# S5 table steps: both sums behind the four products, kernel products ahead of the transposes, forget-gate maps and value copies on ACT

## Chip, cores and metric

One core of one Trainium2 chip. The metric is the device time of one execution in microseconds; the number compared is the median of several runs. Engines: PE is TensorE (matmuls and transposes), ACT is ScalarE, DVE is VectorE, POOL is GpSimd, SP is the engine that only issues transfers here.

## What is computed

A trunk of two residual layers over 512 tokens of width 1024, all in float32. Layer 0 projects the normalised input once (`proj = hn @ w_in`) and feeds an HGRN2 mixer (a gated linear recurrence) and a Mamba-2 mixer; layer 1 has an S5 mixer (a complex diagonal state-space model) and a top-2-of-8 expert SwiGLU. What the change touches is the forget gate of HGRN2 and the preparation of S5:

```python
def hgrn2_mixer(q_pre, ff_pre, fb_pre, i_pre, g_pre, lb, norm_w):
    q = silu(q_pre); v = i_pre
    log_lb, log_1m_lb = log(maximum(lb, LB_FLOOR)), log1p(-lb)
    def forget(f_pre):
        logf = logaddexp(log_lb, log_1m_lb + log_sigmoid(f_pre))
        return logf, -expm1(logf)          # logarithm of the forget gate, and the key
    ...
def _s5_one_direction(ug, a_re, a_im, log_step, b_re, b_im, c_re, c_im):
    # lam = exp(a * delta), one complex number for each of 64 groups x 64 states
    # states by an associative scan over time, outputs from them by c
    ...
```

With s the sigmoid of the pre-activation, the forget gate is `lb + (1 - lb) * s` and the key is `(1 - lb) * (1 - s)`: an affine map each, with a scale and an offset for every channel. The logarithm of the gate is taken after it.

The S5 layer is computed in chunks of 8 time steps. For that the kernel needs, for each of the 64 groups, tables of powers of lam times b (input maps, called BP), powers of lam times c (output maps, CP), and their products (the 15 kernel taps inside a chunk). All depend on parameters alone.

## The kernel before

The order of work is written out by hand; each engine has one in-order program, and they meet on semaphores (`wait_ge`, `then_inc`).

**Blocks and steps.** The first five groups of the projection (ff, fb, q, v, g: forget gates forward and backward, query, value, output gate) are cut into 20 blocks, numbered by `slot`, of 8 block products each (a 128 x 128 weight against 512 columns). The trace shows a block product as two matmul records at L1318. From product 52 (in block 6) to product 160 the table steps of the S5 layer, k = 0 to 31, are threaded between the block products: step k comes ahead of product 52 + floor(k x 108 / 32), thus every 3 or 4 products. A step handles two of the 64 groups.

**A step on DVE** (`powers(k)`): L2837 and L2841 are the two products of BP (512 columns), L2846 adds them; L2850 and L2855 are the two products of CP (576 columns), L2861 adds them. BP and CP have two buffers each, used in turn. BP(k) waits for PE to have transposed and multiplied step k - 2. CP(k) waits for the stores of CP(k - 2) to have landed (`s_cst`). The products are followed by a wait for themselves (`chain.settle()`) ahead of each sum. Behind steps 2 to 5 and 11 to 14 stand four more operations (`logs_in`: the key's map L2816, the gate's map L2818, and the two halves of a split for the logarithm, L2823 and L2825), behind steps 10 and 19 a sum of 2048 columns (`logs_out`, L2829), and behind four later steps the copy of one value block from PSUM (`v_copy`, L2870).

**A step on PE** (`s5_step`): in every fourth step four transposes of a block of C (`c_block`, L1353); then `b_step(k)`, four transposes of BP (L1364); then `kernel_step(k - 1)`, eight small products of BP and CP (L1375).

**A step on ACT**: in every fourth step copies of the C block (`c_copies`, L2153); then two stores of CP(k - 1) (`c_store`, L2182), the copy of the transposed BP (`b_copy`, L2161), its store (L2165), two copies of the kernel taps (`kernel_copy`, L2173) and their store (L2188). At steps 8 and 17 the two logarithms stand behind (`logs`, L2129 and L2130). When the steps of a block are through, `dense_drain(slot)` takes the block's result out of PSUM: two sigmoids for a forget gate (L2120, L2121), Silu for the query (L2123), sigmoid for the output gate (L2125), nothing for the value, which DVE copies. Behind the drain of block 4 ACT copies the first decay tables (L2140), and behind that of block 5 the last ones (L2142, L2143); PE's first C transposes wait for these, and block 6 is behind them in PE's order.

**What follows.** When block 19 is drained, the decay scans of the HGRN2 mixer begin, on ACT (L2262), POOL (L1109, L1112), DVE (L3028) and PE.

**Transfers.** SP loads the weights of the projection in tiles of 1 MB into a ring of six; two tiles are released at about every fourth block's end. The stores of the steps go over ACT's queue.

Of the kernel before, what the change touches and what calls it, by code (L numbers as in the profile page):

```python
# [10 lines left out]
ALU = mybir.AluOpType  # L11
# [42 lines left out]
def build_program(nc, I, out):  # L54
# [27 lines left out]
    with ctx:  # L82
# [68 lines left out]
        add_group("v", w_in, c_v, 512, "tok", "D")  # L151
# [70 lines left out]
        s_k = sem("key_ready")  # L222
# [805 lines left out]
        def _(pool):  # L1028
# [119 lines left out]
            pool.wait_ge(s_lb, HEADS + 1)  # L1148
# [97 lines left out]
        def _(pe):  # L1246
# [76 lines left out]
            def s5_step(k):  # L1323
# [5 lines left out]
                b_step(k)  # L1329
                if k:  # L1330
                    kernel_step(k - 1)

# [125 lines left out]
            def hg_spread(hd):  # L1458
                pe.wait_ge(s_lb, hd + 2)
# [601 lines left out]
        def _(act):  # L2061
# [49 lines left out]
            def dense_drain(slot):  # L2111
# [79 lines left out]
            for slot in range(SLOTS):  # L2191
                for k in steps_of[slot]:
                    if k % 4 == 1 and k < NSTEP - 4:
                        c_copies(k // 4 + 1)
                    if k:
                        c_store(k - 1)
                    b_copy(k)
                    if k:
                        b_store(k - 1)
                        kernel_copy(k - 1)  # L2200
# [15 lines left out]
                elif slot == 5:  # L2216
# [4 lines left out]
                    c_copies(0)  # L2221

# [423 lines left out]
        def _(dve):  # L2646
# [69 lines left out]
            chain.link(dve.tensor_tensor(hgc[:, 7, :], hgc[:, 4, :], hgc[:, 5, :], ALU.subtract))  # L2716
            chain.settle()
# [95 lines left out]
            def logs_in(d, b):  # L2813

                dve.wait_ge(s_drA, cumA[gidx[("ff", "fb")[d]]])
                dve.tensor_scalar(kT[d][:, b, :], kT[d][:, b, :], hgc[:, 6, b:b + 1], hgc[:, 7, b:b + 1],  # L2816
                                  ALU.mult, ALU.add).then_inc(s_k, 1)
                chain.link(dve.tensor_scalar(lf[d][:, b, :], lf[d][:, b, :], hgc[:, 6, b:b + 1], hgc[:, 5, b:b + 1],  # L2818
                                             ALU.mult, ALU.add))
                chain.settle()  # L2820
                if d:
                    dve.wait_ge(s_lf, 1)
                chain.link(dve.tensor_scalar(lnb4[:, b, :], lf[d][:, b, :], 1.0 / LN_SPLIT, 1.0, ALU.mult, ALU.min))  # L2823
                chain.settle()
                dve.tensor_scalar(lf[d][:, b, :], lf[d][:, b, :], LN_SPLIT, None, ALU.max).then_inc(s_lnin, 1)  # L2825
# [5 lines left out]
            def powers(k):  # L2831
# [829 lines left out]
```

## Time and profile before

| | |
|---|---|
| median of 3 runs | 2614.95 us (2611.85 to 2617.03) |
| the profiled execution | 2610.64 us, span 2608.8 us |
| busy share of the span | PE 94%, DVE 65%, ACT 49%, POOL 9% |
| mean granted clock of TensorE | 0.975 of full speed |
| first step's product on DVE (L2837) | 66.69 us |
| last table operation on DVE (L2861) | 229.36 us |
| span of the stretch in question | some 169 us of 2608.8 |

How to read it: the profile is one execution, its times in us from the start of the span. A row of the timeline is one instruction or several merged ones (x2, x8) in order of time. Behind it stands in brackets how long the engine was idle before it and what it waited for. A wait is put down to the event that came last.

### The profile page before, as it was taken

The numbers are of one execution on the slowest core, as the hardware profiler recorded it, in microseconds if no ns is written. First come the engines' busy times: TensorE is split into PE (matmuls) and PEld (weight loads), VectorE is DVE, ScalarE is ACT, GpSimd is POOL, SyncE is SP. The second block draws the span as 40 slices with busy tenths as digits, with TensorE's granted clock in tenths as the row PEclk, the third lists the DMA queues.
The fourth block names the chain that finished last, engine by engine and source line by source line (L and its number), as shares of the span: only waits on it lengthen the run. The fifth ranks groups of instructions, "written<-read, shape, count | busy, mean of one in ns | idle before, by whom it ended". The sixth has DMA issues, their size and how long they took to land.

```text
span 2608.8 us, 31697 instructions
## 1 busy us (share of the span) xinstructions
PE 2458.2 (94%) x12566; PEld 1978.6 (76%) x12566; DVE 1684.6 (65%) x2051; ACT 1281.0 (49%) x1489; POOL 222.5 (9%) x236
## 2 busy tenths in 40 slices
PE   7889998999999999679799999999999999999987
PEld 4445545488888887678599888998899988998866
DVE  6897687322223344693566788668876688667865
ACT  3434434122222223652356676666765577656753
POOL 4114725000000000000100000000000000000010
PEclk9999998999999999789799999999999999999998
DMA  6556411343322223433387799778997799777961
GB/s 169 174 166 203 118 65 41 103 150 96 98 97 98 97 98 113 163 146 106 108 289 242 262 369 354 253 249 296 369 314 249 248 347 369 263 249 263 375 247 50
DMA packets 316386, 526.14 MB, mean 202 GB/s; under 512 B 19286, under 2 KB 175546, under 8 KB 313578
## 3 DMA queue, kind: packets, MB, share of 16 engines
q1 hardware_dynamic: 287162, 479.73, 53.2%
q0 software_dynamic: 5888, 25.78, 3.2%
q10 hardware_dynamic: 23184, 18.55, 2.2%
q8 instruction: 102, 1.67, 0.3%
q14 instruction: 50, 0.41, 0.0%
HBM read 494.46 MB, written 45.81 MB: 207 GB/s over the span
## 4 chain that ended last, share of the span: by engine, by line
PE 81%; DVE 10%; ACT 2%; DMA 2%; issue 2%; POOL 2%; ACTq 0%; POOLq 0%; DVEq 0%
PE psum L1891 28%; PE psum L1405 17%; PE psum L1951 12%; PE psum L1716 5%; PE psum L1953 5%; PE psum L1318 3%; PE psum L1293 2%; PE psum L2051 2%; PE psum L1489 1%; DVE stages L859 1%; DMA s_output_maps_by_state<-stages 1%; DVE stages L869 1%; DVE stages L864 1%; DVE stages L860 1%; POOL stages L1109 1%
## 5 line engine op out<-in xcount | busy, mean ns | idle before, releaser
L3500 DVE TENSOR_TENSOR stages_r<-kept,stages_r 128x2048 fp32r<-128x2048 f32 x336 | 769.3, 2291 | 239.7 <-ACT stages_r L2499 238.5
L2499 ACT ACTIVATE stages_r<-kept 128x2048 fp32r<-128x2048 f32 x336 | 637.6, 1912 | 218.6 <-PE psum L1891 104.1
L1891 PE MATMUL psum<-stages_r 128*128 128x512 f32 x3136 | 738.8, 393 | 3.2 <-issue 3.2
L1891 PEld LDWEIGHTS psum<-stages_r 128*128 128x128 f32 x3136 | 583.7, 188 | 127.0 <-issue 4.8
L1951 PE MATMUL psum<-stages_r 128*128 128x320 f32 x1792 | 465.9, 346 | 4.1 <-DVE stages L3533 3.1
L1405 PE MATMUL psum<-stages_r 128*128 128x512 f32 x1920 | 437.5, 390 | 3.2 <-ACT stages_r L2078 2.7
L1953 PE MATMUL psum<-stages_r 128*128 128x160 f32 x1792 | 423.6, 236 | 0.0
L1405 PEld LDWEIGHTS psum<-stages_r 128*128 128x128 f32 x1920 | 359.9, 188 | 79.5 <-ACT stages_r L2078 3.1
L1953 PEld LDWEIGHTS psum<-stages_r 128*128 128x128 f32 x1792 | 343.5, 192 | 2.0
L1951 PEld LDWEIGHTS psum<-stages_r 128*128 128x128 f32 x1792 | 337.7, 188 | 6.8 <-DVE stages_r L3500 3.8
L3152 DVE TENSOR_TENSOR stages_r<-kept,stages_r 128x2048 fp32r<-128x2048 f32 x54 | 123.8, 2292 | 338.6 <-ACT stages_r L2357 338.6
L2357 ACT ACTIVATE stages_r<-kept 128x2048 fp32r<-128x2048 f32 x54 | 103.5, 1917 | 325.8 <-PE psum L1405 219.1
L1716 PE MATMUL psum<-stages_r,stages_front_r 128*128 128x512 f32 x672 | 152.6, 389 | 0.8 <-issue 0.8
L1716 PEld LDWEIGHTS psum<-stages_r,stages_front_r 128*128 128x128 f32 x672 | 126.1, 188 | 27.3 <-issue 1.2
L1318 PE MATMUL psum<-stages,kept 128*128 128x512 f32 x256 | 118.8, 609 | 0.0
L2537 ACT ACTIVATE stages<-stages 128x160 f32<-128x160 f32 x112 | 37.8, 338 | 159.5 <-DVE stages L3533 159.5
L1318 PEld LDWEIGHTS psum<-stages,kept 128*128 128x128 f32 x256 | 46.9, 192 | 53.8 <-issue 53.8
L1196 POOL DMA_INDIRECT stages<-moe_rows_by_token,stages x8 | 12.3, 1539 | 868.4 <-PE psum L1899 520.4
L3536 DVE TENSOR_TENSOR kept<-stages 128x160 f32<-128x160 f32 x112 | 36.6, 327 | 45.2 <-ACT stages L2537 45.2
L2064 ACT ACTIVATE stages<-kept 128x1024 f32<-128x1024 f32 x24 | 25.3, 1055 | 77.5 <-DVE kept L3146 49.9
L1489 PE MATMUL psum<-stages,kept 128*128 128x512 f32 x128 | 59.4, 594 | 0.0
L1293 PE MATMUL psum<-kept,stages 128*128 128x512 f32 x128 | 57.7, 613 | 0.8 <-DVE stages L3139 0.8
(439 smaller groups left out, 2470.0 us busy)
## 6 DMA issues: line engine op xcount, KB each, us to landing
kept<-in_moe_w_gu_dram SPq DMA_DIRECT2D x224, 1024.0 KB, 7.1
kept<-in_moe_w_down_dram SPq DMA_DIRECT2D x112, 1024.0 KB, 6.5
kept<-in_ffn_w_gu_dram SPq DMA_DIRECT2D x28, 1024.0 KB, 5.2
kept<-in_ev_w_in_dram SPq DMA_DIRECT2D x16, 1024.0 KB, 7.3
kept<-in_ffn_w_down_dram SPq DMA_DIRECT2D x14, 1024.0 KB, 5.0
s_output_maps_by_state<-stages ACTq DMA_DIRECT2D x64, 128.0 KB, 2.0
s_input_maps<-stages ACTq DMA_DIRECT2D x32, 256.0 KB, 2.5
s_output_maps<-s_output_maps_by_state SPq DMA_DIRECT2D x32, 256.0 KB, 4.9
```

What stands on the lines that cost most here:

```text
L1293: m = pe.matmul(psum[:, b0 + b, 0:width], act[:, 4 * kk + k, b * P:(b + 1) * P], w[:, k, 0:width], **at)
L1318: m = pe.matmul(psum[:, b, :], *pair, start=kk == 0 and k == 0, stop=kk == 1 and k == 3)
L1405: m = pe.matmul(psum[:, 4 * (g % 2) + b, :], *pair, start=kk == 0 and k == 0 and n == 0, stop=kk == 1 and k == 3 and n == 2, skip_group_ch ...
L1489: m = pe.matmul(bank, w[:, k, b * P:(b + 1) * P], hnT[:, n, :], **at)
L1716: m = pe.matmul(psum[:, 2 * c + hf, :], a[:, k, at], w[hf][:, k, :], start=j == 0 and k == 0 and n == 0, stop=j == FJ - 1 and k == 3 and n ...
L1891: m = pe.matmul(out_, a, b, start=start and n == 0, stop=stop and n == len(pairs) - 1, skip_group_check=True)
L1951: pe.matmul(bank[:, 0:2 * CAP], wh[:, k, fs], x_[:, k, :], start=k == 0, stop=False, skip_group_check=True)
L1953: m = pe.matmul(bank[:, 0:CAP], wl[:, k, fs], x_[:, k, 0:CAP], start=False, stop=k == 7, skip_group_check=True)
L2357: act.activation(f_high[t % 2], ring[:, n % RING, :].rearrange("p (k n) -> p k n", k=4), ACT.Copy).then_inc(s_wh, 1)
L2499: act.activation(w_high[n % WSLOTS], unit_tile(n), ACT.Copy).then_inc(s_wh, 1)
L3152: dve.tensor_tensor(f_low[t % 2], ring[:, (SPLIT_RUNS[run][1] + t) % RING, :].rearrange("p (k n) -> p k n", k=4), f_high[t % 2], ALU.subtr ...
L3500: dve.tensor_tensor(w_low[n % WSLOTS], unit_tile(n), w_high[n % WSLOTS], ALU.subtract).then_inc(s_ws, 1)
```

## The change

It moves work and reorders it; nothing is computed that was not before.

- `powers(k)`: all four products come first, then the sum of BP, then the sum of CP. A wait for the finished sum of the step before stands ahead of each second product, since BQ and CQ, the scratch buffers of the second products, are single.
- `logs_in` becomes `logs_of`: its two split operations are put inside the next step's `powers`, one behind the BP products and one behind the CP products (steps 3 to 6 and 12 to 15).
- The two affine maps of `logs_in` go to ACT as `bounded_forget(d, b)`, behind the drains of blocks 4 to 11 (and behind the decay copies in blocks 4 and 5).
- The value copies go to ACT as drains of blocks 12 to 15.
- PE does `kernel_step(k - 1)` ahead of `b_step(k)`, and ACT does `kernel_copy(k - 1)` ahead of `b_copy(k)`.

```diff
-        add_group("v", w_in, c_v, 512, "tok", "D")
+        add_group("v", w_in, c_v, 512, "tok", "A")
...
                     c_block(k // 4 + 1)
-                b_step(k)
                 if k:
                     kernel_step(k - 1)
+                b_step(k)
...
                 name, bank = groups[g][0], psum[:, b, :]
-                if name == "v":
-                    return
                 act.wait_ge(s_grp, 4 * g + b + 1)
...
+                elif name == "v":
+                    act.wait_ge(s_lam, 16)
+                    act.activation(vtok[:, b, :], bank, ACT.Copy).then_inc(s_drA, 1)
...
+            def bounded_forget(d, b):
+
+                act.wait_ge(s_lb, 2)
+                act.wait_ge(s_drA, cumA[gidx[("ff", "fb")[d]]] - 3 + b)
+                act.activation(lf[d][:, b, :], lf[d][:, b, :], ACT.Identity, scale=hgc[:, 6, b:b + 1], bias=hgc[:, 5, b:b + 1])
+                act.activation(kT[d][:, b, :], kT[d][:, b, :], ACT.Identity, scale=hgc[:, 6, b:b + 1], bias=hgc[:, 7, b:b + 1]).then_inc(s_k, 1)
...
                     if k:
                         c_store(k - 1)
+                    if k:
+                        kernel_copy(k - 1)
                     b_copy(k)
                     if k:
                         b_store(k - 1)
-                        kernel_copy(k - 1)
...
                     c_copies(0)
+                if 4 <= slot < 12:
+                    bounded_forget(slot // 4 - 1, slot % 4)
...
-            def logs_in(d, b):
...
+            def logs_of(d, b):
+
+                split_done = []
+
+                def logs_split():
+                    dve.wait_ge(s_k, 4 * d + b + 1)
+                    if d:
+                        dve.wait_ge(s_lf, 1)
+                    chain.link(dve.tensor_scalar(lnb4[:, b, :], lf[d][:, b, :], 1.0 / LN_SPLIT, 1.0, ALU.mult, ALU.min))
+                    split_done.append(chain.n)
+
+                def logs_floor():
+                    dve.wait_ge(chain.sem, split_done[0])
+                    dve.tensor_scalar(lf[d][:, b, :], lf[d][:, b, :], LN_SPLIT, None, ALU.max).then_inc(s_lnin, 1)
+
+                return logs_split, logs_floor
...
-            def powers(k):
+            def powers(k, behind=None):
...
+                if k:
+                    dve.wait_ge(s_bc, 2 * k - 1)
...
-                chain.settle()
-                dve.tensor_tensor(BP[k % 2], BP[k % 2], BQ, ALU.add).then_inc(s_bc, 1)
+                inputs_done = chain.n
+                if behind is not None:
+                    behind[0]()
                 dve.wait_ge(s_cc, k // 4 + 1)
...
+                if k:
+                    dve.wait_ge(s_bc, 2 * k)
...
-                chain.settle()
+                outputs_done = chain.n
+                if behind is not None:
+                    behind[1]()
+                dve.wait_ge(chain.sem, inputs_done)
+                dve.tensor_tensor(BP[k % 2], BP[k % 2], BQ, ALU.add).then_inc(s_bc, 1)
+                dve.wait_ge(chain.sem, outputs_done)
                 dve.tensor_tensor(CP[k % 2], CP[k % 2], CQ, ALU.add).then_inc(s_bc, 1)
...
-                powers(k)
+                powers(k, logs_behind)
+                logs_behind = None
...
-                        logs_in(d, k - LOGS_IN[d])
+                        logs_behind = logs_of(d, k - LOGS_IN[d])
...
-                for b in range(4):
-                    if k == steps_of[4 * gv + b + 1][0]:
-                        v_copy(b)
```

The semaphore `s_lb` gets one more increment, behind the last of the four constants of the maps (`hgc`), and its later waits count one further; one more wait between these constants and the table work goes.

## Rows read from the trace of the kernel before

**Rows 1.** Timeline of DVE, step 3 with logarithms: start, length, engine, line.
```profile
88.46 0.69 DVE L2837 TENSOR_TENSOR stages<-stages,kept 128x512 f32<-128x512 f32 x1
89.06 0.69 DVE L2841 TENSOR_TENSOR stages<-stages 128x512 f32<-128x512 f32 x1
89.78 0.69 DVE L2846 TENSOR_TENSOR stages<-stages 128x512 f32<-128x512 f32 x1
90.39 0.75 DVE L2850 TENSOR_TENSOR stages<-stages 128x576 f32<-128x576 f32 x1
91.06 0.75 DVE L2855 TENSOR_TENSOR stages<-stages 128x576 f32<-128x576 f32 x1
91.84 0.76 DVE L2861 TENSOR_TENSOR stages<-stages 128x576 f32<-128x576 f32 x1
92.52 0.59 DVE L2816 TENSOR_SCALAR stages<-stages,kept 128x512 f32<-128x512 f32 x1
...
94.06 0.43 DVE L2825 TENSOR_SCALAR stages<-stages 128x512 f32<-128x512 f32 x1
94.40 0.69 DVE L2837 TENSOR_TENSOR stages<-stages,kept 128x512 f32<-128x512 f32 x1
```

**Rows 2.** Timeline of PE, steps 30 and 31.
```profile
224.47 0.60 PE L1364 MATMUL psum<-kept,stages 128*128 128x128 f32 x4
...
225.00 0.62 PE L1375 MATMUL psum<-stages 128*16 128x128 f32 x8
...
225.55 2.84 PE L1318 MATMUL psum<-stages,kept 128*128 128x512 f32 x6
...
228.23 0.60 PE L1364 MATMUL psum<-kept,stages 128*128 128x128 f32 x4
```

**Rows 3.** Groups by line, 80 to 236 us: count, busy us, mean ns, idle before.
```profile
L2829 DVE TENSOR_TENSOR stages<-stages 128x2048 f32<-128x2048 f32 x2 | 4.6, 2284 | 0.0
...
L2870 DVE COPY stages<-psum 128x512 f32<-128x512 f32 x4 | 2.7, 683 | 0.0
```

**Rows 4.** Timeline from the decay copies to step 2.
```profile
65.94 1.56 ACT L2140 ACTIVATE stages<-psum 64x256 f32<-64x256 f32 x4 [8.18 <-PE psum L1343]
...
71.18 0.66 PE L1353 MATMUL psum<-kept,stages 128*128 128x128 f32 x4 [3.63 <-ACT stages L2143]
...
84.48 0.76 DVE L2850 TENSOR_TENSOR stages<-stages 128x576 f32<-128x576 f32 x1 [0.94 <-DMA s_output_maps_by_state<-stages]
```

**Rows 5.** Groups by line on ACT, 0 to 450 us.
```profile
L2278 ACT ACTIVATE stages<-stages 128x512 f32<-128x512 f32 x10 | 6.3, 626 | 0.0
...
L2292 ACT ACTIVATE stages<-stages,kept 128x512 f32<-128x512 f32 x6 | 3.9, 711 | 0.0
```

**Rows 6.** Timeline behind the first logarithms.
```profile
124.59 1.28 ACT L2123 ACT_TABLE_LOAD   x1
...
128.24 0.62 PE L1375 MATMUL psum<-stages 128*16 128x128 f32 x8 [2.55 <-ACT stages L2173]
```

**Rows 7.** Windows: length, then busy us (count) of PE, PEld, DVE, ACT, POOL; clock, DMA share, GB/s.
```profile
66.00:75.00 9.00, 5.25 (x21) 2.84 (x19) 5.04 (x13) 5.67 (x16) 2.34 (x1) 0.85 0.65 197
...
205.00:235.00 30.00, 28.87 (x130) 13.55 (x129) 25.95 (x39) 11.12 (x25) 5.80 (x9) 1.00 0.45 141
```

**Rows 8.** Step 24's wait, and the DMA issues of 191 to 194 us with median landing.
```profile
199.10 0.76 DVE L2850 TENSOR_TENSOR stages<-stages 128x576 f32<-128x576 f32 x1 [2.15 <-DMA s_output_maps_by_state<-stages]
...
kept<-in_ev_w_in_dram SPq DMA_DIRECT2D x1, 1024.0 KB, 7.3
s_output_maps_by_state<-stages ACTq DMA_DIRECT2D x2, 128.0 KB, 6.2
```

**Rows 9.** Timeline: transposes of steps 7, 11 and 16, and POOL's first scan operation.
```profile
112.47 0.66 PE L1364 MATMUL psum<-kept,stages 128*128 128x128 f32 x4
...
132.33 0.60 PE L1364 MATMUL psum<-kept,stages 128*128 128x128 f32 x4
...
160.09 0.60 PE L1364 MATMUL psum<-kept,stages 128*128 128x128 f32 x4
...
237.06 1.51 POOL L1109 TENSOR_TENSOR stages<-stages 128x512 f32<-128x512 f32 x1 [2.09 <-ACT stages L2280]
```

More of the change, by code:

```diff
@@ L221, in build_program @@
         s_lf = sem("log_forget_ready")
-        s_k = sem("key_ready")
+        s_k = sem("forget_and_key_ready")
         s_lnin = sem("ln_inputs_ready")
@@ L1147, in _ @@
             pool.wait_ge(s_gram, 2 * PAIR_SLOTS)
-            pool.wait_ge(s_lb, HEADS + 1)
+            pool.wait_ge(s_lb, HEADS + 2)
             masked_decays(0)
@@ L1458, in hg_spread @@
             def hg_spread(hd):
-                pe.wait_ge(s_lb, hd + 2)
+                pe.wait_ge(s_lb, hd + 3)
                 if hd == 1:
@@ L2715, in _ @@
             chain.settle()
-            chain.link(dve.tensor_tensor(hgc[:, 7, :], hgc[:, 4, :], hgc[:, 5, :], ALU.subtract))
-            chain.settle()
+            dve.tensor_tensor(hgc[:, 7, :], hgc[:, 4, :], hgc[:, 5, :], ALU.subtract).then_inc(s_lb, 1)
             dve.wait_ge(s_sin, 3)
@@ L2811, in _ @@
                 m.then_inc(s_rc, 1)
-            def logs_in(d, b):
[L2815 to L2819, printed above, removed]
-                chain.settle()
[L2821 to L2825, printed above, removed]
+            def logs_of(d, b):
[10 more added lines that the diff above has]
+                return logs_split, logs_floor
             def logs_out(d):
@@ L2844, in powers @@
                                                  [P, STEP, 2 * L5, GC]), ALU.mult))
-                chain.settle()
-                dve.tensor_tensor(BP[k % 2], BP[k % 2], BQ, ALU.add).then_inc(s_bc, 1)
+                inputs_done = chain.n
+                if behind is not None:
+                    behind[0]()
                 dve.wait_ge(s_cc, k // 4 + 1)
@@ L2859, in powers @@
                                                  [P, 2 * STEP, M5, GC]), ALU.mult))
-                chain.settle()
+                outputs_done = chain.n
[4 more added lines that the diff above has]
+                dve.wait_ge(chain.sem, outputs_done)
                 dve.tensor_tensor(CP[k % 2], CP[k % 2], CQ, ALU.add).then_inc(s_bc, 1)
@@ L2864, in _ @@
             dve.wait_ge(s_s5in, 64)
[L2865 to L2870 removed]
+            logs_behind = None
             for k in range(NSTEP):
[L2873 removed]
+                powers(k, logs_behind)
+                logs_behind = None
                 for d in range(2):
                     if LOGS_IN[d] <= k < LOGS_IN[d] + 4:
[L2876 removed]
+                        logs_behind = logs_of(d, k - LOGS_IN[d])
                     if k == LOGS_OUT[d]:
                         logs_out(d)
[L2879 to L2881 removed]
             def diag_scores(hd):
```

5 lines of the change are left out of this document (removed).

## Prediction

> **What bounds the kernel now.** All the changed work lies in one stretch, from about 66 to 235 us, where blocks of the first projection (PE) are interleaved with 32 steps that build the tables of the S5 layer. A step k is: six DVE operations (two products and their sum for the inputs, BP; the same for the outputs, CP), four transposes and eight small products on PE, three copies on ACT, two stores of CP. I read the stretch first as windows, then as instructions in order of time.
>
> On DVE a step with the four logarithm operations lasts 5.94 us, from one L2837 to the next; without them it is 92.52 - 88.46 = 4.06 us [rows 1]. PE's own work for a step of three block products is 228.23 - 224.47 = 3.76 us, 0.53 of it transposes and 0.55 small products [rows 2]; two of the records at L1318 are one block product, 0.855 us, so a step of four takes 4.61. There are 108 block products in 32 steps (3.375 each), so PE wants 3.76 + 0.375 x 0.855 = 4.08 us, and some 0.5 more in seven of the steps, for four more transposes (C block): 4.2 on average. So DVE and PE are level in the ordinary steps, and DVE alone sets the pace in the eight steps with logarithms, in two with a 2.28 us sum behind them [rows 3], and in four with a copy of v. What is taken off DVE in an ordinary step is therefore worth next to nothing. That is the main thing to see: savings must be counted only where DVE is late.
>
> **The change, part by part.** In DVE's order, from [rows 1]: a 512-wide product that follows independently starts 0.60 to 0.61 after the one before it, a 576-wide one 0.67; the sums, which wait for their second factor, start after 0.72 and 0.78. With both sums last those waits are gone: 0.12 + 0.11 = 0.23 us a step, 7.4 in all, and a step is 3.8. Of the four logarithm operations two leave DVE and two lose their wait: 94.40 - 92.52 = 1.88 becomes 2 x 0.34 = 0.68 (0.34 is 94.06 to 94.40, an independent follower). That is 1.20 x 8 = 9.6. The v copies are 0.683 long [rows 3], 0.61 net of overlap: 2.4. Gross 19.4 us off DVE.
>
> Against this, four things.
>
> *The start.* The first map for block 4 stands on ACT behind the first decay copies and ahead of block 5's drain and the last decay copies. PE waits for those: 3.63 us before its C transposes at 71.18 [rows 4]. ACT is busy from 65.94 until then, so the maps lengthen this wait by their whole length. No map with a scale and a bias from memory is in the trace. The nearest rows: 0.626 with neither (L2278), 0.711 with one (L2292) [rows 5]. From below 0.60, by the plain one; from above 0.91, if the second operand cost twice the first's 0.085 and more; I take 0.626 + 2 x 0.085 = 0.80, less 0.08 overlap: 0.72 each, 1.4 us for the pair. The start is 1.4 us later (1.0 to 1.8). I assume no table load between Sigmoid or Silu and these maps, since the plain copies between them have none; if each cost 1.28 [rows 6] both ways, 2.6 more at the start.
>
> The mean granted clock in this window is 0.85 [rows 7], so part of it ran at the lower level (1.2 GHz), after that 3.6 us of waiting; I count nothing for a wait of 5.0.
>
> The Trainium skill ("ScalarE: Activation LUTs", section "What ACT_TABLE_LOAD costs") gives some 93 ns for each pointer operand, which makes 0.80 us, as by the rows. In "Table sets" it says that identity lies in every set: by that no load comes. Its "Rules for kernel authors" there speak against the change: multiply and add belong on VectorE. No row here sets the same map on both engines.
>
> *PE now waits for stores.* The sum for BP stood ahead of the CP products; now it stands behind them, and the first CP product waits until the store of CP of two steps before has landed. So far such a wait cost DVE 0.94 at step 2, and 2.15 at step 24, where the stores landed after 6.2 us beside a 1 MB weight tile that took 7.3 [rows 4, 8]. Four steps have landings like these (5.3 to 6.2 us), all beside tiles. PE passed the waits by; now it inherits them, less a slack: DVE may start BP(k) once the products of k - 2 are done, one step ahead of PE; BP's sum ends 3.3 us after that start, and PE's transposes come at 4.2. Slack 0.9 in an ordinary step, 0.2 in one with logarithms.
>
> *ACT at step 10.* ACT's logarithms end at 124.59, then come a table load, block 9's drain, C copies, the input copy and the kernel copies, for which PE waited 2.55 us, to 128.24 [rows 6]. The kernel copies now come ahead of the input copy (0.5 earlier), but a pair of maps stands ahead of both (1.4 later).
>
> *PE's order.* Kernel products ahead of the transposes: no work more, and while DVE's sum is awaited PE does them. It hides the late sum (1.3 + 0.7 us later in the step) in ordinary steps.
>
> **The sum, by the starts of PE's transposes of step k**, before [rows 9, 2] against after:
> - Step 2: CP(2) waits for the first store, issued behind PE's C transposes, so it starts at 84.48 + 1.4 = 85.9; BP(3) at 88.5.
> - Steps 3 to 6 at 3.81 + 0.68 = 4.49: BP(7) at 106.45, transposes at 109.75 against 112.47: 2.7 ahead.
> - Steps 7 to 9 run at PE's pace, as before. Step 10: ACT's logarithms follow step 8, 2.7 earlier, with 0.7 of kernel copies gone from between: 124.59 - 3.4 = 121.2; load 1.28, drain 0.5, maps 1.4, C copies 0.6, kernel copies 0.7: 125.6. Kernel products, then transposes at 126.25.
> - Step 11: 126.25 + 4.56 = 130.8 against 132.33: only 1.5 ahead.
> - Steps 12 to 15 (4.49 by DVE, 3.8 to 4.6 by PE), with 1.5 for a store behind the next pair of tiles (issue near 141.5 + 5.8 to landing, against a CP(15) due at 145.8); step 16 at 154.4 against 160.09: 5.7 ahead.
> - Steps 16 to 31: PE needs 15 x 3.76 + 5 x 0.855 + 3 x 0.5 = 62.2. Add 1.0 for the 2.28 us sum beyond the slack, 0.3 for ACT's second logarithms, 2.5 for the third pair of tiles (2.15 as now, with DVE some 0.5 earlier): 66.0, against 68.1 before. Step 31 at 220.4 against 228.23: 7.8 ahead.
> - The last step's products already stand ahead of its transposes: 0.5 to 0.8.
>
> Total 8.5 us, say 9. The decay scans on POOL, ACT and DVE that follow start when the last block is drained (POOL's first at 237.06 [rows 9]), and nothing in them is touched; I carry the gain through to the end undiminished. The profiled execution took 2610.64 us (span 2608.8), so about 2601.9; the median of the runs shown is 4.3 us above it, and the forecast is against that: 2614.95 - 9 = **2606 us**.
>
> **The rivals.** *(a) PE hardly waits.* Store and ACT delays fall beside other waits; what counts is 19.4 gross less 1.4 at the start and about 2 where PE is the bound: 16, **2599**. For it: ACT is busy only 11.12 us of the last 30 of the stretch [rows 7]. Against: steps 7 to 10 show PE's own pace already.
> *(b) The gain is given back to ACT and stores.* The C copies stand ahead of a store in seven steps; such a store made DVE wait 0.94 at step 2 [rows 4]; with half the slack gone 0.5 x 7 = 3.5. Another 2.5 if maps and drains hold up the kernel copies also in blocks 8, 10 and 11. 8.5 - 6 = 2.5: **2612**, no measurable change (0.2%, 5.2 us, is about what runs of this kernel can tell). The skill's rule for multiply and add, named above, would lead here if anywhere.
> *(c) Slower, by the store chain.* A landing of 6.2 us cost DVE 2.15; with DVE some 0.5 earlier 2.7, and if several come in a row no slack is left for PE. The same bytes in less time could slow more landings: at five more the gain is gone and 5.0 beyond (8.5 - 13.5), from where on the kernel is slower by over 0.2%; with seven, 8.5 - 18.9 = -10.4: **2625**. Against: the DMA engines' share is 0.45 at the stretch's end [rows 7], and the four slow landings sit beside tile loads, of which there are no more than before.
> *(d) Nothing happens*: no; DVE is late in eight steps beyond doubt.
>
> **How the numbers follow.** Forecast case 0.45 (its own range 2602 to 2609.5), (a) 0.19, (b) 0.28, (c) 0.08. Faster by over 0.2%: 0.64; within: 0.28; slower: 0.08. The range reaches from 2597, two below (a), to 2614, taking in (b) with the upper bounds of the maps and the start; it leaves out (c) and the lower tail of (a).
>
> **What would show it.** Right: L2837 to L2837 at 4.5 to 4.8 us in the log steps; PE's wait ahead of 71 us grown from 3.6 to about 5; PE waiting for the new BP sum at steps 2, 10, 15 and 24; maps of 0.80 us without table loads; DVE's busy time in the stretch down by some 11 us (16 scalar operations and four copies); POOL's first scan operation near 228 instead of 237. Wrong: table loads between the maps; PE waiting in every step for the sum behind CP; store landings over 5 us in more than four steps; or a later stage that takes back what this one gave.

## Result: slower, 1.0049 of the time before

The changed kernel takes 2625.87 us (2624.91 to 2626.73, five runs) against 2614.95, a ratio of 1.0049 with a 95% interval of 1.0038 to 1.0059. The forecast was 2606, with a range to 2614. The profiled execution's span is 14.9 us longer than before's; that execution of before lay 4.3 us under its own median, which is most of the difference between 14.9 and the medians' 10.9.

The page of the changed kernel (span; busy time of each engine; granted clock in 40 slices):

```profile
span 2623.7 us, 31703 instructions
...
PE 2461.3 (94%) x12566; PEld 1979.8 (75%) x12566; DVE 1669.5 (64%) x2031; ACT 1294.8 (49%) x1509; POOL 243.4 (9%) x236
...
PEclk9899999999999999889899999999999999999998
```

DVE did 15 us less and nothing got faster. GpSimd has the same 236 instructions and 21 us more busy time (222.5 before); more on that line below. The timeline of the changed kernel, start to step 6 (BP's products are now L2850 and L2856, CP's L2866 and L2873, the sums L2882 and L2884; the maps L2132 and L2133):

```profile
67.62 0.81 ACT L2132 ACTIVATE stages<-stages,kept 128x512 f32<-128x512 f32 x1
68.34 0.80 ACT L2133 ACTIVATE stages<-stages,kept 128x512 f32<-128x512 f32 x1
...
72.81 1.12 PE L1353 MATMUL psum<-kept,stages 128*128 128x128 f32 x4 [5.18 <-ACT stages L2151]
...
88.31 0.68 DVE L2850 TENSOR_TENSOR stages<-stages,kept 128x512 f32<-128x512 f32 x1
...
92.80 0.68 DVE L2850 TENSOR_TENSOR stages<-stages,kept 128x512 f32<-128x512 f32 x1
...
102.10 0.76 DVE L2866 TENSOR_TENSOR stages<-stages 128x576 f32<-128x576 f32 x1 [3.21 <-DMA s_output_maps_by_state<-stages]
...
103.78 0.69 DVE L2882 TENSOR_TENSOR stages<-stages 128x512 f32<-128x512 f32 x1
...
104.52 1.12 PE L1364 MATMUL psum<-kept,stages 128*128 128x128 f32 x4 [3.56 <-DVE stages L2882]
105.43 6.01 PE L1318 MATMUL psum<-stages,kept 128*128 128x512 f32 x8
...
111.92 0.33 PE L1364 MATMUL psum<-kept,stages 128*128 128x128 f32 x1
```

Up to step 4 this is the forecast: maps of 0.80, a wait of 5.18 (5.0 forecast; 3.63 in [rows 4]), BP(3) at 88.31 (88.5 forecast), a step with logarithms of 4.49 us where [rows 1] have 5.94. Then CP(5) waits 3.21 us for a store and BP's sum, now behind it, comes at 103.78. PE has nothing else to do and waits 3.56. Its next transposes take 1.12 us instead of 0.66, and eight records of block products 6.01 us: PE runs at half clock. Before, the same eight took 3.70, and step 6's transposes stood at 108.57; now 111.92. Behind the first logarithms it happens again:

```profile
127.87 1.28 ACT L2124 ACT_TABLE_LOAD   x1
...
131.69 0.76 DVE L2866 TENSOR_TENSOR stages<-stages 128x576 f32<-128x576 f32 x1 [5.25 <-ACT stages L2161]
...
132.45 1.04 PE L1375 MATMUL psum<-stages 128*16 128x128 f32 x8 [4.25 <-ACT stages L2181]
```

PE's wait is 4.25 where [rows 6] have 2.55, and the load comes 3.3 us later than before instead of 3.4 earlier. The transposes of steps 16 and 31, and GpSimd's first scan operation, which answer to [rows 9] and [rows 2]:

```profile
167.76 0.66 PE L1364 MATMUL psum<-kept,stages 128*128 128x128 f32 x4
...
241.89 0.66 PE L1364 MATMUL psum<-kept,stages 128*128 128x128 f32 x4
...
250.15 1.50 POOL L1109 TENSOR_TENSOR stages<-stages 128x512 f32<-128x512 f32 x1 [1.62 <-ACT stages L2291]
```

Step 16 is 7.7 us late against before, step 31 13.7, the scan 13.1. Nearly all of the loss is made inside the stretch: 13.1 us of the 14.9 between the two profiles stand at the scan. The waits of 56 to 250 us, and windows (columns as in [rows 7]):

```profile
PE psum L1364 <- DVE stages L2882: 20.5, 13, 4.1
ACT stages L2181 <- DMA s_kernels<-stages: 24.6, 8, 7.4
DVE stages L2866 <- DMA s_output_maps_by_state<-stages: 19.0, 8, 4.6
...
102.00:112.00 10.00, 7.48 (x21) 3.53 (x22) 7.56 (x13) 3.12 (x6) 0.66 (x1) 0.66 0.25 73
130.00:138.00 8.00, 5.22 (x17) 2.91 (x18) 6.31 (x8) 4.21 (x10) 3.23 (x2) 0.57 0.44 139
...
80.00:235.00 155.00, 129.42 (x571) 63.23 (x570) 120.95 (x190) 71.70 (x136) 33.87 (x29) 0.92 0.48 149
```

The same of the kernel before:

```profile
PE psum L1364 <- DVE stages L2846: 15.7, 10, 2.3
...
DVE stages L2850 <- DMA s_output_maps_by_state<-stages: 3.6, 3, 2.1
...
102.00:112.00 10.00, 8.26 (x38) 3.98 (x38) 9.79 (x17) 4.44 (x8) 0.77 (x2) 1.00 0.48 145
...
80.00:235.00 155.00, 134.09 (x620) 64.92 (x619) 143.58 (x220) 65.76 (x131) 20.27 (x33) 1.00 0.53 163
```

DVE's busy time from 80 to 235 us fell from 143.6 to 121.0, but it now waits for stores of CP eight times, 19.0 us in place of 3.6. PE's waits for DVE's sum of BP grew less in total, from 15.7 to 20.5 us, than in length: the longest was 2.3 and is 4.1. The mean granted clock over the 155 us is 0.92, which is some 24 us at half clock; before it was 1.00.

### The profile page after: what moved, and what is told of

Its sections match the earlier page's. It is cut to its first block, busy times and chain, and to the rows that moved or that the text cites. A ratio compares the mean times of both kernels' runs of the same rounds, so it can differ in the third digit from the quotient of the medians.

```text
span 2623.7 us, 31703 instructions
## 1 busy us (share of the span) xinstructions
PE 2461.3 (94%) x12566; PEld 1979.8 (75%) x12566; DVE 1669.5 (64%) x2031; ACT 1294.8 (49%) x1509; POOL 243.4 (9%) x236
## 4 chain that ended last, share of the span: by engine, by line
PE 81%; DVE 9%; ACT 3%; DMA 3%; POOL 2%; issue 2%; ACTq 0%; POOLq 0%; DVEq 0%
PE psum L1891 28%; PE psum L1405 16%; PE psum L1951 12%; PE psum L1716 5%; PE psum L1953 5%; PE psum L1318 4%; PE psum L1293 2%; PE psum L2051 2%; DMA s_output_maps_by_state<-stages 1%; PE psum L1489 1%; DVE stages L859 1%; DVE stages L869 1%; DVE stages L864 1%; DVE stages L860 1%; POOL stages L1109 1%
```

## The experiments

Each time stands beside runs of the kernel before on the same chip; the ratio is to those. "Changed" is the changed kernel.

### Which part of the change

**e1: the sum early again.** BP's sum goes back ahead of CP's products, behind the split operation; all else stays.
```diff
                 if behind is not None:
                     behind[0]()
+                dve.wait_ge(chain.sem, inputs_done)
+                dve.tensor_tensor(BP[k % 2], BP[k % 2], BQ, ALU.add).then_inc(s_bc, 1)
...
-                dve.wait_ge(chain.sem, inputs_done)
-                dve.tensor_tensor(BP[k % 2], BP[k % 2], BQ, ALU.add).then_inc(s_bc, 1)
```


> The changed kernel with one thing undone: the sum of BP stands ahead of the CP products again (behind the first split operation), everything else as changed. Theory S (PE inherits the waits for the stores of CP, and its long waits bring the lower clock): PE's waits of 3.6 to 4.1 us at steps 5, 15 and 24 shrink to under 2, of the five stretches at 1.2 GHz the three behind these steps go, and the time falls by 10 to 18 us, to 2608 to 2616. Rival A (the maps on ACT hold up its copies, and these the rest): the time stays within 4 us of 2626, for ACT's work is unchanged. Rival O (kernel copies ahead of the input copy wait for kernel stores and hold all up): the same, 2626.

Measured 2610.39, ratio 0.9989 (0.9979 to 0.9999). DVE still waits for stores (10.1 us, six times), but PE waits for a BP sum only 4.8 us; step 31's transposes come 12 us earlier than in the changed kernel. The late sum is the part that loses.

**e2: maps and value copies back on DVE**, the new orders kept.
```diff
-        add_group("v", w_in, c_v, 512, "tok", "A")
+        add_group("v", w_in, c_v, 512, "tok", "D")
...
-                if 4 <= slot < 12:
-                    bounded_forget(slot // 4 - 1, slot % 4)
```


> The changed kernel with the maps and the value copies back on DVE, all orders as changed (sums behind four products, kernel products and kernel copies first). Theory S: DVE's log steps are slower again (about 5.5 us), which gives the stores time there, but the waits at steps 18 to 26 reach PE as before: 2616 to 2622, with one to three stretches at 1.2 GHz. Rival A: all of the loss was ACT's, 2608 to 2613. Rival O: 2620 to 2630.

Measured 2617.43, ratio 1.0018 (1.0008 to 1.0027): the new orders alone lose.

**e3: maps and value copies on ACT alone**, with the sums and the orders of PE and ACT as in the kernel before.
```diff
-                dve.wait_ge(s_drA, cumA[gidx[("ff", "fb")[d]]])
-                dve.tensor_scalar(kT[d][:, b, :], kT[d][:, b, :], hgc[:, 6, b:b + 1], hgc[:, 7, b:b + 1],
-                                  ALU.mult, ALU.add).then_inc(s_k, 1)
+                act.activation(kT[d][:, b, :], kT[d][:, b, :], ACT.Identity, scale=hgc[:, 6, b:b + 1], bias=hgc[:, 7, b:b + 1]).then_inc(s_k, 1)
```


> The kernel before with only the maps and the value copies moved to ACT; the sums, PE's order and ACT's order as before. Theory S: the start is 1.6 us later, the log steps are 1.1 to 1.3 us shorter until the stores bound them, PE doesn't wait for stores: 2606 to 2612, faster than before. Rival A: slower than before, 2618 to 2626. Rival O: like S.

Measured 2611.85, ratio 0.9995 (0.9985 to 1.0005): no difference, where the expectation had a gain. What leaves DVE comes back as waits of PE at the start (5.2 us) and at step 10 (3.7).

**e4: the old orders of PE and ACT** (transposes first, input copy first) with the late sum.
```diff
-                if k:
-                    kernel_step(k - 1)
                 b_step(k)
+                if k:
+                    kernel_step(k - 1)
```


> The changed kernel with PE's transposes ahead of the kernel products and ACT's input copy ahead of the kernel copies again; sums behind all four products and maps on ACT as changed. Theory S: PE's transposes wait for the late sum in every step and the kernel products stand behind them, so no better than the changed kernel: 2624 to 2634. Rival O: the loss goes, 2608 to 2615. Rival A: 2622 to 2628.

Measured 2630.36, ratio 1.0065 (1.0046 to 1.0084), the slowest of all. Its waits:

```profile
PE psum L1364 <- DVE stages L2881: 26.6, 19, 4.4
DVE stages L2849 <- PE psum L1375: 25.2, 28, 2.1
```

DVE waits for PE's small products in 28 steps and PE for DVE's sum in 19: a closed ring. So the new orders on PE and ACT are needed by the late sum, as the forecast said of PE's, and are not the loss.

### The waits and the clock

**e5: three CP buffers** in the changed kernel, so that CP(k) waits for the store of step k - 3. The room comes from BQ, which moves to a row of norm weights that is free then.
```diff
-        CP = [rga.take(2 * STEP * M5 * GC).rearrange(stepv, g=STEP, d=2, m=M5) for _ in range(2)]
+        CP = [rga.take(2 * STEP * M5 * GC).rearrange(stepv, g=STEP, d=2, m=M5) for _ in range(3)]
...
-                if k >= 2:
-                    dve.wait_ge(s_cst, 32 * (k - 1))
+                if k >= 3:
+                    dve.wait_ge(s_cst, 32 * (k - 2))
```


> The changed kernel with three buffers of CP in place of two (the scratch of BP moves to a norm weight row that is free at that time), so that CP(k) waits for the stores of k - 3; all orders and ACT's work as changed, with BP's sum still behind all four products. Theory S (the waits for the stores of CP reach PE through the late sum): PE's waits at steps 5, 15, 18, 21 and 24 go, the one at step 10 for ACT's kernel copies stays; 2608 to 2616. Rival A (ACT's load or its order is the cause): within 3 us of 2626. Rival L (the late sum itself costs, whatever the stores do): the same, 2622 to 2627.

Measured 2612.15, ratio 0.9992 (0.9979 to 1.0005). This takes back all the change lost, but no gain shows, although DVE waits for no CP store any more. PE waits instead 6.3, 3.0 and 3.4 us for kernel copies at steps 10, 16 and 21.

**e6: useless products in PE's waits**, five ahead of the first C transposes and four each in steps 5, 10, 15 and 24.
```diff
+                if k in FILLED_STEPS:
+                    pe.wait_ge(s_big, k - 1)
+                    fill(psum[:, 4 + k % 2, :], FILLED_STEPS[k])
                 if k:
                     kernel_step(k - 1)
                 b_step(k)
```


> The changed kernel with work added on PE: 5 useless products (ident against a chunk of 512 columns, 0.855 us each, into a bank that is overwritten next) in the wait ahead of the first C transposes, and 4 each ahead of PE's part of steps 5, 10, 15 and 24. Nothing else changes; the waits themselves are as long. Theory C (each of the five stretches at 1.2 GHz behind these waits costs 1.7 to 3.4 us of its own): the stretches go or shrink, and the kernel with more work is 6 to 13 us faster than the changed one, 2613 to 2620. Rival: the lower clock ran in the shadow of DVE and the stores; 2625 to 2630.

Measured 2616.33, ratio 1.0015 (1.0005 to 1.0026): 21 products more, 9.5 us less than the changed kernel. A window of it, and PE at step 5 (L1327 are the useless ones; two records are one product):

```profile
102.00:112.00 10.00, 9.39 (x48) 4.25 (x46) 9.57 (x18) 6.28 (x12) 1.35 (x2) 1.00 0.41 130
...
98.89 3.60 PE L1327 MATMUL psum<-stages,kept 128*128 128x512 f32 x8
...
103.12 0.66 PE L1373 MATMUL psum<-kept,stages 128*128 128x128 f32 x4
103.61 3.60 PE L1318 MATMUL psum<-stages,kept 128*128 128x512 f32 x8
...
107.69 0.66 PE L1373 MATMUL psum<-kept,stages 128*128 128x128 f32 x4
```

CP(5) waits for its store as long as in the changed kernel (3.17 us), but the products behind take 3.60 us and not 6.01. Step 5's transposes come 1.4 us earlier, from the start's products, and step 6's 4.2. So the lower clock costs time of its own, here 9.5 us in all. Not all of that is loss against the kernel before: the 1.4 us at the start belong to a stretch of lower clock that it has too (granted clock from 66 to 80 us: 0.88 before, 0.76 changed, 1.00 here). Nor is all of it shown to be the clock's alone, since DVE's waits for stores fell along with it, from 19.0 to 14.8 us.

**e7: early sum and three CP buffers** (e1 and e5 together).

> e1 (BP's sum ahead of the CP products, the rest as changed) with three buffers of CP. Theory S: DVE's waits for the stores at steps 4, 15, 23 and 24 go (7 to 8 us together in e1), PE's and ACT's at step 10 stay: 2602 to 2608, faster than before. Rival (what bounds e1 is PE and ACT, and DVE's waits are hidden): 2609 to 2612.

Measured 2608.77, ratio 0.998 (0.997 to 0.9989). This lies between the two ranges of the expectation and decides for neither.

**e8: as e7, and two pairs of maps moved**: block 4's behind the decay and C copies, block 9's behind block 10's steps.
```diff
+                if slot == 10:
+                    bounded_forget(1, 1)
...
-                if 4 <= slot < 12:
+                if slot == 5:
+                    bounded_forget(0, 0)
+                if 4 < slot < 12 and slot != 9:
                     bounded_forget(slot // 4 - 1, slot % 4)
```


> e7 with the maps of block 4 behind block 5's decay and C copies, and those of block 9 behind the steps of block 10, so that neither stands ahead of what PE waits for. The start is 1.4 us earlier, step 10's kernel copies 1.4 us earlier, and the first stretch at 1.2 GHz is 3.4 in place of 6.8 us. Theory A' (the maps cost where they stand on the path, and nothing elsewhere): 3 to 6 us less than e7, 2597 to 2604. Rival: the same as e7.

Measured 2603.95, ratio 0.9966 (0.9955 to 0.9977), faster than either kernel. So the place of the two pairs costs some 5 us (4.8 between the medians).

### The kernel stores: a theory that fell

In e5 to e8 ACT still waits at its kernel copies, and the waits name the kernel store as releaser (24.6 us in the changed kernel). That copy now stands ahead of the input copy. The theory was that it waits for the store of two steps before to land; a third kernel stage would end that.

**e9: the kernel before with a third CP buffer and a third kernel stage**, as a control.
```diff
+        KJ.append(nw[:, 0, 512:512 + STEP * 15 * GC].rearrange("p (g j c) -> p g j c", g=STEP, j=15))
...
-                if k >= 2:
-                    act.wait_ge(s_kst, 16 * (k - 1))
+                if k >= 3:
+                    act.wait_ge(s_kst, 16 * (k - 2))
```


> The kernel before, with a third CP buffer and a third kernel stage and nothing else. Theory S (the change lost its gain because it carries store waits to PE; before mostly hides them): before waits for stores only 3.6 us in the stretch from 80 to 236 and its kernel copies wait for none that its waits list, so the buffers give it little: 2608 to 2614, step 31's transposes at 225 to 228 against 228.23. Rival B (the extra buffers are worth the same to either kernel, and the experiments with them say nothing about the change): 2600 to 2604, as far below the kernel before as three CP buffers took the changed one (14 us).

Measured 2607.86, ratio 0.9983 (0.9974 to 0.9993): the buffers give the kernel before a little as well, but not the 14 us that the third CP buffer gives the changed one.

**e10: the changed kernel with both.**

> The changed kernel with three CP buffers and a third kernel stage as well. With three CP buffers alone it took 2612.2, and PE still waited 6.3, 3.0 and 3.4 us for kernel copies that waited for kernel stores (step 31 at 228.46). Theory S2 (that second store chain, opened by the kernel copy ahead of the input copy on ACT, took the rest of the forecast gain): those waits go, step 31 at 220 to 224, 2602 to 2608, and the forecast's 2606 is met once no store holds anything up. Rival A (ACT's own work beside the logs and sigmoids bounds steps 10, 15 and 20, and the store wait is only the last of several): 2610 to 2613, as with three CP buffers.

Measured 2613.29, ratio 1.0004 (0.9994 to 1.0013). The number is close to rival A's, and theory S2 fell: the third stage gave nothing over e5. But ACT isn't busy in those waits either.

**e11: e8 with a third kernel stage.**

> The version with the early sum, three CP buffers and the maps of blocks 4 and 9 out of the way (2604.0), and a third kernel stage. Theory S2: its waits for kernel stores (22.7 us in the stretch, of which 3.1 at step 6 and 3.5 at step 14 reach PE) go: 2597 to 2601, step 31 at 213 to 216 against 219.18. Rival A: 2602 to 2605, unchanged.

Measured 2603.0, ratio 0.9965 (0.9953 to 0.9978): unchanged from e8.

**e12: e11 with the late sum.**

> The same as the run before it with BP's sum behind all four products, as in the changed kernel: the late sum alone, where no store waits are left for it to carry. Forecast of the late sum's worth from the trace of before: DVE's step 4.10 to 3.86 us, so over the 20-odd steps that DVE sets, up to 4 us faster than that run. Rival L (the late sum loses even without stores, since PE's transposes start 0.7 us later in a step and it closes the ring over PE's kernel products): the same or up to 5 us slower than that run.

Measured 2606.93, ratio 0.9983 (0.9973 to 0.9992): 3.9 us slower than e11 instead of up to 4 faster, as rival L had it.

The timeline of e10 from 143 us, three engines, tells what both theories missed (L1081 is GpSimd's add of the skip term, L2197 the kernel store):

```profile
143.37 12.64 POOL L1081 TENSOR_TENSOR stages<-stages 16x32 f32<-16x32 f32 x2 [4.87 <-ACT stages L2182]
...
154.97 0.74 DVE L2885 TENSOR_TENSOR stages<-stages 128x576 f32<-128x576 f32 x1
155.84 0.33 ACTq L2197 DMA_DIRECT2D s_kernels<-stages  x1
...
157.27 0.36 ACT L2182 ACTIVATE kept<-psum 16x240 f32<-16x240 f32 x1 [8.90 <-DMA s_kernels<-stages]
...
159.30 0.69 DVE L2851 TENSOR_TENSOR stages<-stages,kept 128x512 f32<-128x512 f32 x1 [3.59 <-PE psum L1376]
```

The row holds two adds of 16x32 elements. Such an add takes 0.23 us when alone; the first of these took 12.44 and ended at 155.81. DVE has run without a gap all that time; its last sum ends at 155.71. Within 0.13 us of that ACT issues the kernel store, which waits for this add. Everything behind that store in ACT's order has stood still: CP stores, kernel copy, input copy. The releaser named by the waits, the kernel store, is only the instruction in ACT's order that was stuck. The changed kernel has the same while DVE is at steps 19 to 21 (L1080 the add, L2196 the kernel store, L2190 the CP store):

```profile
180.12 9.06 POOL L1080 TENSOR_TENSOR stages<-stages 16x32 f32<-16x32 f32 x2 [6.51 <-ACT stages L2181]
...
188.21 0.68 DVE L2856 TENSOR_TENSOR stages<-stages 128x512 f32<-128x512 f32 x1
191.92 0.76 DVE L2866 TENSOR_TENSOR stages<-stages 128x576 f32<-128x576 f32 x1 [3.03 <-DMA s_output_maps_by_state<-stages]
...
182.69 0.60 ACT L2169 ACTIVATE stages<-psum 128x512 f32<-128x512 f32 x1
189.02 0.33 ACTq L2196 DMA_DIRECT2D s_kernels<-stages  x1
189.44 0.90 ACTq L2190 DMA_DIRECT2D s_output_maps_by_state<-stages  x2
```

DVE stops at 188.89 for a CP store that ACT couldn't issue until GpSimd's first add was done, after 8.86 us. The store landed 1.9 us after its issue; it was not slow, it was late. Of DVE's 19.0 us of waits for stores, 11.2 (CP(5), CP(15), CP(24)) are for three stores that landed 6.7 to 7.5 us after their issue, beside weight tiles, and 7.8 for five that landed 2.0 to 3.1 us after theirs. The groups by line, 80 to 235 us, first of the kernel before, then of the changed one:

```profile
L1080 POOL TENSOR_TENSOR stages<-stages 16x32 f32<-16x32 f32 x32 | 18.5, 577 | 142.5 <-ACT stages L2173 140.6 <-DMA s_output_maps_by_state<-stages 1.9
```
```profile
L1080 POOL TENSOR_TENSOR stages<-stages 16x32 f32<-16x32 f32 x29 | 33.9, 1171 | 128.9 <-ACT stages L2181 128.9
```

The mean doubles. The kernel before has no add over 2.3 us: its sums wait 0.12 and 0.11 us for their factors in every step. The change closed these gaps, and not by the late sums alone: the split operations fill them too. In e1, with the early sum, an add begins in a step with logarithms (L1080 the add, L2864 the sum of BP, L2831 the split ahead of it):

```profile
104.20 6.77 POOL L1080 TENSOR_TENSOR stages<-stages 16x32 f32<-16x32 f32 x1 [3.45 <-ACT stages L2181]
...
106.31 0.42 DVE L2831 TENSOR_SCALAR stages<-stages 128x512 f32<-128x512 f32 x1
106.65 0.68 DVE L2864 TENSOR_TENSOR stages<-stages 128x512 f32<-128x512 f32 x1
...
110.19 0.69 DVE L2856 TENSOR_TENSOR stages<-stages 128x512 f32<-128x512 f32 x1
110.91 0.69 DVE L2864 TENSOR_TENSOR stages<-stages 128x512 f32<-128x512 f32 x1
```

At 106.65 the sum follows without a gap and the add goes on; at 110.91 there is no split operation, the sum waits for its factor, and the add ends, at 110.97. In e11, also with the early sum, the longest add takes 10.3 us. In e4, where DVE waits for PE in nearly every step, it is 0.84.

### The add moved

Each of the next six runs moves the add to DVE, ahead of BP's products of a later step, when its operand is long there:
```diff
-            def add_skip(k):
-                pool.wait_ge(s_kc, k + 1)
-                m = KJ[k % 2][0:GC, :, L5 - 1, :]
-                pool.tensor_tensor(m, m, Dm[0:GC, STEP * k:STEP * (k + 1), :], ALU.add).then_inc(s_kd, 1)
...
+            def add_skip(k):
+                dve.wait_ge(s_kc, k + 1)
+                m = KJ[k % 2][0:GC, :, L5 - 1, :]
+                dve.tensor_tensor(m, m, Dm[0:GC, STEP * k:STEP * (k + 1), :], ALU.add).then_inc(s_kd, 1)
...
                     dve.wait_ge(s_kk, k - 1)
+                if k >= 3:
+                    add_skip(k - 3)
```

**e13: in the changed kernel, alone.**

> The changed kernel with the skip term's add (16x32, 0.23 us on GpSimd when it is alone) moved to VectorE, ahead of the next step's products; nothing else. Theory G (VectorE without gaps keeps GpSimd out of its add, up to 9.1 us in the changed kernel, and ACT's in-order queue stands behind that add): ACT's waits at the kernel copies fall from 24.6 us to under 8; the CP stores' waits stay and still reach PE, as do the low-clock stretches: 2612 to 2620. Rival K (the kernel stores' landings are what ACT waits for): no change, 2622 to 2628, or up to 3 us more for the adds on VectorE.

Measured 2619.91, ratio 1.0026 (1.0016 to 1.0036): 6 us less than the changed kernel. ACT's waits behind kernel stores fell from 24.6 to 14.0 us; theory G had expected under 8. What the rest waits for wasn't separated.

**e14: in the changed kernel with three CP buffers and three kernel stages.**

> The changed kernel with three CP buffers, a third kernel stage and the skip add on VectorE. Theory G: no wait of ACT, VectorE or PE for a store or for GpSimd is left, so the forecast's own sum holds, less nothing for stores and plus some 3 us for 32 small adds: step 31's copy at 220 to 225 against 228.99, 2600 to 2608. Rival A (ACT's own work bounds steps 10, 15 and 20): 2610 to 2614, unchanged from the same kernel with the add on GpSimd (2613.3).

Measured 2601.12, ratio 0.9956 (0.994 to 0.9973), against 2613.29 with the add on GpSimd. ACT's longest wait at a kernel copy fell from 9.0 us to 5.7; the expectation had no such wait left, but PE still waits 5.7 us in all for kernel copies (12.9 in e10). Step 31's transposes and the first scan operation:

```profile
218.06 0.66 PE L1356 MATMUL psum<-kept,stages 128*128 128x128 f32 x4
...
226.20 1.51 POOL L1101 TENSOR_TENSOR stages<-stages 128x512 f32<-128x512 f32 x1 [1.39 <-ACT stages L2283]
```

**e15: in e12 (late sum, maps moved, all buffers).**

> The version with the late sum, both buffers and the maps of blocks 4 and 9 out of the way (2606.9), with the skip add on VectorE. Theory G: its two long waits of ACT (9 us at steps 15 and 20, at the ends of adds of 12.65 and 9.67 us) go: 2595 to 2602. Rival A: 2605 to 2610.

Measured 2596.99, ratio 0.9941 (0.9924 to 0.9957), the fastest of all.

**e16: in e8 (early sum, maps moved, three CP buffers).**

> The best version so far (early sum, three CP buffers, maps out of the way: 2604.0), with the skip add on VectorE. Theory G: adds of 7.8 and 7.5 us on GpSimd put ACT behind at steps 6 and 14 (PE waited 3.1 and 3.5 us there): 2597 to 2602. Rival A: 2603 to 2608, the adds' own time on VectorE being the only effect.

Measured 2600.92, ratio 0.9955 (0.9939 to 0.9972). By the medians the late sum, 3.9 us slower than the early one with the add on GpSimd (e12 against e11), is 3.9 us faster with the add on DVE (e15 against this; a third kernel stage, also in e15, was worth 1 us or nothing elsewhere). That would make the sign of the late sum hang on the add; the intervals of both pairs overlap, so it is likely, not shown. Against e8 the moved add gives 3 us at most here: ACT's waits behind kernel stores didn't fall (22.7 us in e8, 25.7 here), and PE still has a wait of 3.5 us, at 145.5.

**e17: in e9, the kernel before with all buffers.**

> The kernel before, with the third CP buffer, the third kernel stage and the skip add on VectorE. Theory D (the change's own gain is what the forecast worked out, some 6 to 9 us, once none of its waits are in the way): 2606 to 2611, since the buffers alone gave 2607.9 and in it GpSimd's add never took over 2.3 us; the changed kernel with the same three is then 6 to 9 us faster. Rival E (the gain is the mends' own, whichever kernel they are put into): 2600 to 2603.

Measured 2608.96, ratio 0.9985 (0.9975 to 0.9994): as e9. In the kernel before the add cost nothing that can be seen. The same three mends leave before at 0.9985 and the changed kernel at 0.9956, so with them the change itself is worth 0.0029, some 7.6 us; by the two intervals it can be anything from nearly nothing to 14.

**e18: in e5, the changed kernel with three CP buffers and two kernel stages.**

> The changed kernel with three CP buffers and the skip add on VectorE, but two kernel stages. Theory G (GpSimd's add, not the kernel stores' landing, was what ACT stood behind): 2601 to 2606, near the 2601.1 with the third kernel stage; ACT's waits for kernel stores under 15 us. Rival K (the landings bind as well): 2608 to 2612, as with three CP buffers and the add on GpSimd.

Measured 2602.07, ratio 0.9956 (0.9939 to 0.9973). Two mends suffice. From 2625.9: the third CP buffer alone gives 13.7 us, the moved add alone 6.0, both 23.8, more than their sum; one explanation is that each wait hid part of the other. ACT's waits behind kernel stores are 20.5 us (44.9 in e5), not under 15 as expected: the time is theory G's, this sign of it is not.

## Why the prediction was wrong

Its arithmetic of the work was right. *Off DVE*: 15.1 us less busy time in the whole execution, where some 11 were forecast (the 22.6 us less from 80 to 235 us count also the steps that have fallen behind that window); a step with logarithms takes the 4.49 us forecast. *Maps*: 0.80, no table loads between them. *The start*: 72.81 against 71.18, 1.6 later where 1.4 was forecast. *Steps 2 to 4*: CP(2) at 85.65 (85.9), BP(3) at 88.31 (88.5). *PE's order*: needed, as e4 shows. *Later stages*: the scan operation moved with step 31. *The sum*: 8.5 us, which the mended pair of kernels (e14, e17) gives as 7.6. That the two come so close is in part luck: the interval is wide, and e14 still pays for the maps' place, which e8 prices at 5 us. One small slip: 2610.64 less 9 is 2601.6 and not 2601.9; the forecast of 2606 doesn't use it.

The step that failed is **"PE now waits for stores"**: its charge for the waits and its slack were too small, and two terms beside it were put at nothing.

- *The slack and the count.* The forecast charged two further store waits, 1.5 at step 15 and 2.5 at step 24, less a slack of 0.9 or 0.2. The changed kernel has eight waits of CP for stores, 19.0 us, and PE's waits for the sum behind them reach 4.1 us. Already CP(5) waits 3.21 us: it is due at 98.9, the store of step 3 was issued at 94.9, beside a weight tile that took 7.0 us, and is down at 102.0. Before, that store was issued at 94.3 and down at 100.1, 2.2 us ahead of CP(5), which came at 102.28 by itself, as DVE was slower. So the first gain ran into a store that had been hidden, and PE was behind the sum. Rival (c) had this place and this price, 2625, and a chance of 0.08; that it met the number is luck, for it asked for more slow landings, and those over 5 us are in three steps (in five before). e1 and e5 take the loss away from either end.
- *The clock.* "I count nothing for a wait of 5.0." PE waited 3.56 us at step 5 and 4.25 at step 10, and the windows there have granted clocks of 0.66 and 0.57 where before has 1.00. The useless products of e6 put the price of all such stretches at some 9.5 us, the one at the start among them. [Rows 7] had shown the clock at 0.85 behind a wait of 3.6, the one wait of that size in the stretch; the forecast read it and didn't ask which other waits would grow to it.
- *The add on GpSimd.* It is in no part of the prediction. The list of what DVE's gaps were good for had PE and stores in it, not a third engine. The change takes 0.23 us of gaps out of every step; the add then lasts up to 8.9 us, and ACT's queue behind it sends out CP stores late, which are DVE's next wait. Moving the add is worth 6.0 us in the changed kernel (e13) and 12.2 where the buffers are there (e10 against e14).

The Trainium skill bears on the last one: "SBUF — State Buffer", section "Who interferes with whom", says that a VectorE instruction with two SBUF inputs contends with a GpSimd one that reads SBUF, and that their shared port pair is an exclusive lock. These traces agree and go further: what the add waits through is not one instruction of 0.7 us, but all that follow each other without a gap. That the shared port is the means was not tried by itself; shown is that the long adds end when DVE pauses, and that moving them shortens ACT's longest waits.

Of TensorE's clock the Trainium skill ("TensorE: Matmul & The Clock Gate", section "What's actually happening") gives two levels, 1.2 and 2.4 GHz. The traces agree with two: four transposes took 1.12 us at the lower one and 0.66 at the full one.

What stays open: whether the start's loss (PE waits 5.18 us there, and 0.76 is the mean clock of 66 to 80 us) and step 10's can be mended further than in e15, how the loss divides between the three, and what ACT's remaining waits behind kernel stores (17.5 us in e14) are for.

## What to carry to other kernels

When work is taken off an engine, ask what its gaps were serving: a store that lands just in time, and here a tiny GpSimd operation in the middle of a chain. Move an operation out of such a chain before you close the gaps. And when a producer's result is put behind an instruction that can wait, charge every consumer the whole wait, count behind each long wait of PE a stretch at half clock as well (in e6 up to 2.8 us for one), and give the buffer a third copy first. A mechanism worth 12 us in one version was worth nothing in another, so a control with the same mends in the old kernel is needed before a part of a change is called good or bad.

## What the runs showed of the hardware

- GpSimd's 16x32 add took 0.23 us alone, and up to 8.9, 11.6 and 12.4 us (changed, e5, e12) while VectorE ran SBUF operations back to back; in the kernel before, with gaps of 0.12 and 0.11 us in each step, it took 2.3 at most.
- PE's granted clock fell to the lower level beside its waits of 3.6 to 5.2 us in the changed kernel, and didn't beside those of 2.3 and 2.6 us in the kernel before. The length of the wait doesn't settle it: in e10 a wait of 2.2 us at 102 has the lower clock beside it and one of 3.8 us at 128 has not. Useless products in such waits made the kernel faster (e6). Windows of e10:

```profile
102.50:106.50 4.00, 4.00 (x16) 2.19 (x11) 3.53 (x7) 3.38 (x7) 0.40 (x1) 0.57 0.55 168
128.00:136.00 8.00, 7.53 (x37) 3.97 (x38) 6.17 (x10) 5.46 (x11) 1.40 (x3) 1.00 0.45 142
```

- A scale and a bias both read from SBUF cost ACT 0.80 to 0.81 us for 128x512, against 0.626 with neither and 0.711 with one [rows 5].
